# A two-block model on one core: the weight units moved to other byte phases, the memory's additions and transposes placed further apart

## The reference

```python
def hybrid_layer(x, mem_n, ...):            # twice
    h = layer_norm(ALPHA * x + 0.5 * swiglu(x, ffn1_w_gu, ffn1_w_down), ln_g[0], ln_b[0])
    (dn_q, dn_k, dn_v, dn_b, dn_a, dn_z, sw_q, sw_k, sw_v, xa_q, gates) = split(h @ w_in)
    o_dn = deltanet_branch(...)             # chunked gated delta rule, 4 heads of 128
    o_sw = sliding_window_attention(sw_q, sw_k, sw_v, swa_sinks)
    o_xa = memory_cross_attention(xa_q, mem_n, w_mem_kv)
    merged = sum(sigmoid(gates) * (branches @ w_branch))
    h = layer_norm(ALPHA * h + merged @ w_out, ln_g[1], ln_b[1])
    return layer_norm(ALPHA * h + 0.5 * swiglu(h, ffn2_w_gu, ffn2_w_down), ln_g[2], ln_b[2])

def first_block(x, mem, ...):
    mem_n = layer_norm(mem, mem_ln_g, mem_ln_b)          # 256 x 1024
    for l in range(2): x = hybrid_layer(x, mem_n, ...)

def second_block(x, ...):                   # once
    x = x + token_mixer(rmsnorm(x, g), ...) # four attention variants, gates, w_out
    x = x + conv_ffn(rmsnorm(x, g), ...)    # 1024 -> 5632 -> 1024
    return rmsnorm(x, norm_final_g)
```

## Time and profile before

| | |
|---|---|
| time, median of 3 runs | 3506.49 us (3505.77 to 3510.85) |
| the profiled execution's own time | 3508.38 us, granted clock 0.997 |
| its span | 3506.6 us |
| PE busy | 3446.7 us (98%), 19244 matmuls |
| DVE, ACT busy | 2226.2 us (63%), 1676.8 us (48%) |
| DMA | 358.88 MB, mean 102 GB/s |

### The profile page before, as it was taken

The page is one execution under the profiler, slowest core; times in us unless marked ns, Lnnn a source line. Parts: engine busy times, 40 slices in busy tenths (PEclk is TensorE's granted clock), DMA queues, the critical chain, the costliest instruction groups (busy, mean ns, idle before and its releaser), DMA issues.

```text
span 3506.6 us, 49704 instructions
## 1 busy us (share of the span) xinstructions
PE 3446.7 (98%) x19244; PEld 2934.4 (84%) x19244; DVE 2226.2 (63%) x4226; ACT 1676.8 (48%) x3230; POOL 111.5 (3%) x132
## 2 busy tenths in 40 slices
PE   9999999999999999999999999999999999999999
PEld 7998888877889998999888877888987777788887
DVE  5566565556685667566755566774766777666653
ACT  5355454554354445444555544453545444444432
POOL 0010000000000100010000000000100000000000
PEclk9999999999999999999999999999999999999999
DMA  5464321112334643464221112254632222233332
GB/s 154 134 172 148 121 88 52 45 52 64 97 99 135 172 130 104 131 168 136 91 72 46 46 58 84 94 136 137 168 118 76 67 70 82 73 96 96 97 99 88
DMA packets 197140, 358.88 MB, mean 102 GB/s; under 512 B 21982, under 2 KB 25215, under 8 KB 196904
## 3 DMA queue, kind: packets, MB, share of 16 engines
q1 hardware_dynamic: 177704, 321.34, 29.1%
q0 software_dynamic: 18432, 33.56, 5.7%
q10 hardware_dynamic: 768, 0.79, 0.1%
HBM read 353.23 MB, written 4.74 MB: 102 GB/s over the span
## 4 chain that ended last, share of the span: by engine, by line
PE 90%; DVE 6%; ACT 3%; issue 1%; DMA 0%; DVEq 0%; SPq 0%; ACTq 0%
PE bank L2491 20%; PE bank L2500 20%; PE bank L2492 20%; PE bank L2526 6%; PE bank L2529 6%; PE bank L2528 6%; PE bank L2479 2%; PE bank L2474 1%; PE bank L2569 1%; PE bank L2662 1%; DVE w_lo L3235 1%; PE bank L2672 1%; DVE page_r L3277 1%; PE bank L2537 1%; PE bank L2589 1%
## 5 line engine op out<-in xcount | busy, mean ns | idle before, releaser
L2491 PE MATMUL bank<-page_r,w_hi 128*128 128x512 f32 (+1 forms) x3446 | 1368.2, 397 | 27.7 <-DVE w_lo L3235 21.9
L2500 PE MATMUL bank<-page_r,w_lo 128*128 128x512 f32 (+1 forms) x3446 | 1343.8, 390 | 0.0
L2492 PE MATMUL bank<-page_r,w_hi 128*128 128x512 f32 (+1 forms) x3446 | 1332.4, 387 | 0.0
L2491 PEld LDWEIGHTS bank<-page_r,w_hi 128*128 128x128 f32 x3446 | 650.0, 189 | 174.5 <-DVE w_lo L3235 23.1
L2815 ACT ACTIVATE w_hi<-raw 128x512 fp32r<-128x512 f32 x864 | 532.4, 626 | 515.0 <-PE bank L2500 506.7
L2500 PEld LDWEIGHTS bank<-page_r,w_lo 128*128 128x128 f32 x3446 | 649.4, 188 | 129.0
L2492 PEld LDWEIGHTS bank<-page_r,w_hi 128*128 128x128 f32 x3446 | 650.2, 189 | 125.6 <-issue 3.8
L3235 DVE TENSOR_TENSOR w_lo<-raw,w_hi 128x512 fp32r<-128x512 f32 x864 | 574.6, 686 | 141.1 <-ACT w_hi L2815 139.1
L2526 PE MATMUL bank<-page_r,w_hi 128*128 128x256 f32 x1792 | 507.3, 283 | 2.4 <-DVE w_lo L3253 2.4
L2528 PE MATMUL bank<-page_r,w_hi 128*128 128x256 f32 x1792 | 507.1, 283 | 0.0
L2529 PE MATMUL bank<-page_r,w_lo 128*128 128x256 f32 x1792 | 507.1, 283 | 0.0
(11 more groups left out here) (321 smaller groups left out, 3437.4 us busy)
## 6 DMA issues: line engine op xcount, KB each, us to landing
raw<-weights SPq DMA_DIRECT2D x864, 256.0 KB, 2.6
raw<-pairs SPq DMA_DIRECT2D x320, 256.0 KB, 3.1
raw<-pairs POOLq DMA_DIRECT2D x128, 256.0 KB, 5.8
bias_rows<-bias_row SPq DMA_DIRECT2D x8, 320.0 KB, 4.4
page_f<-x_t SPq DMA_DIRECT2D x8, 256.0 KB, 5.5
page_f<-bias_rows SPq DMA_DIRECT2D x8, 256.0 KB, 4.6
out_t<-page_f SPq DMA_DIRECT2D x12, 128.0 KB, 1.8
cst<-consts SPq DMA_DIRECT2D x4, 272.0 KB, 3.6
```

The source lines that it names most:

```text
L2491: self.e.matmul(o, hi, X.hi[kt], start=first, stop=False)
L2492: self.e.matmul(o, hi, X.lo[kt], start=False, stop=False)
L2500: last = self.e.matmul(o, lo, X.hi[kt], start=False, stop=final)
```

## The change

Three things. First, units get 32 floats between them (`PITCH`), `small` shrinks to make room, and each unit is placed when it is taken: a slab's unit at the start of its pitch plus 28 floats, plus 32 more where its number is odd; a unit of a Strassen pair at plus 20 floats; a unit lent as a page at plus 0. The room shifts the pages too: they now start at phase 0. All slab units start at phase 240 (16 bytes short of a page's phase), pair units at phase 64 or 192. The wide instructions on two units now have two runs of 512 with a gap. Second, the layer norm of the memory yields twice after each of its seven additions, and each value projection waits six steps instead of one between its copy and its transposes. Third, the bias row is written from two pages by two DMAs.

```diff
+SMALL = 1184
+UNIT_START = 28
+SLAB_PHASE = (0, 32)
+PAIR_PHASE = 20
 CONST_PARTS = 4
 NGAIN = 48
 UNIT = SLAB * P
+PITCH = UNIT + 32
...
-        super().__init__(region[:, at * UNIT:(at + 1) * UNIT], rounded[:, at * UNIT:(at + 1) * UNIT])
+        super().__init__(None)
         self.at, self.region, self.rounded, self.landed, self.loads = at, region, rounded, landed, 0
         self.added, self.adds = added, 0
+        self.place(0)
+
+    def place(self, phase):
+
+        self.phase, a = phase, UNIT_START + self.at * PITCH + phase
+        self.f, self.r = self.region[:, a:a + UNIT], self.rounded[:, a:a + UNIT]
+        return self
+
+    def for_slab(self):
+
+        return self.place(SLAB_PHASE[self.at % 2])
+
+    def for_pair(self):
+
+        return self.place(PAIR_PHASE)
+
+    def two(self, region):
+        a = UNIT_START + self.at * PITCH
+        both = region[:, a:a + 2 * PITCH].rearrange("p (u c) -> p u c", u=2)
+        return both[:, :, self.phase:self.phase + UNIT]
 
     def wide(self):
-        return self.region[:, self.at * UNIT:(self.at + 2) * UNIT]
+        return self.two(self.region)
 
     def wide_rounded(self):
-        return self.rounded[:, self.at * UNIT:(self.at + 2) * UNIT]
+        return self.two(self.rounded)
...
-            slot = lender.take()
+            slot = lender.take().place(0)
...
-        with nc.sbuf_tensor("w_lo", [P, NRAW * UNIT], F32R) as lo:
+        with nc.sbuf_tensor("w_lo", [P, NRAW * PITCH + 64], F32R) as lo:
             self.w_lo = lo
-        self.raw = sb("raw", [P, NRAW * UNIT])
-        with nc.sbuf_tensor("w_lent", [P, NHI * UNIT], F32) as lent:
+        self.raw = sb("raw", [P, NRAW * PITCH + 64])
+        with nc.sbuf_tensor("w_lent", [P, NHI * PITCH + 32], F32) as lent:
             self.w_lent = lent
-        self.w_hi = sb("w_hi", [P, NHI * UNIT], F32R)
+        self.w_hi = sb("w_hi", [P, NHI * PITCH + 32], F32R)
...
-        self.small = sb("small", [P, 2048])
+        self.small = sb("small", [P, SMALL])
...
-            unit = self.raws.take()
+            unit = self.raws.take().for_slab()
...
-            raw, hi = self.slab[self.next_round] = [self.slab[self.next_round][0], self.his.take()]
+            raw, hi = self.slab[self.next_round] = [self.slab[self.next_round][0], self.his.take().for_slab()]
...
-        k.will(vector="s1 s2 s3 s4 s5 s6 s7")
-        self.tiles_sum(k, s, tiles, landed, n)
+        for m in range(1, 8):
+            k.will(vector=f"s{m}")
+            self.tiles_sum(k, s, tiles, landed, n, m)
+            yield
+            yield
         for _ in range(6):
...
-        out = s1, s3 = self.raws.take_pair()
+        out = s1, s3 = [x.for_pair() for x in self.raws.take_pair()]
...
                         self.memory_out(k, b, q, 0)
                         self.banks.give(b, k["out"])
-                        yield
+                        for _ in range(6):
+                            yield
...
-        self.bias_store(k, row)
+        self.bias_store(k, p, p2)
+        self.pages.give(p, (self.m.s_row, 32))
+        self.pages.give(p2, (self.m.s_row, 32))
...
-    def tiles_sum(self, k, s, tiles, landed, n):
-        self.clear(s)
-        self.wait_ge(*landed[0])
-        self.wait_ge(*landed[1])
-        self.e.tensor_tensor(s.cols(n), tiles[0].cols(n), tiles[1].cols(n), ALU.add).then_inc(k.lane.vector, 1)
-        for m in range(2, 8):
-            self.wait_ge(*landed[m])
+    def tiles_sum(self, k, s, tiles, landed, n, m):
+        self.wait_ge(*landed[m])
+        if m == 1:
+            self.clear(s)
+            self.wait_ge(*landed[0])
+            self.e.tensor_tensor(s.cols(n), tiles[0].cols(n), tiles[1].cols(n), ALU.add).then_inc(k.lane.vector, 1)
+        else:
             self.wait_ge(*k[f"s{m - 1}"])
             self.e.tensor_tensor(s.cols(n), s.cols(n), tiles[m].cols(n), ALU.add).then_inc(k.lane.vector, 1)
...
+        self.wait_ge(*k["wide"])
+        self.e.dma_start(self.m.row[:, 0:SEQ], p.f[0:8, :]).then_inc(self.m.s_row, 16)
         self.wait_ge(*k["narrow"])
-        self.e.dma_start(self.m.row, row[0:8, :]).then_inc(self.m.s_row, 16)
+        self.e.dma_start(self.m.row[:, SEQ:640], p2.f[0:8, 0:P]).then_inc(self.m.s_row, 16)
```

More of the change, by code:

```diff
@@ L538, in small @@
         self.small_at += n
-        assert a + n <= 2048
+        assert a + n <= SMALL
         return self.m.small[:, a:a + n]
@@ L916, in prepare @@
         add("a11", s3)
-        a11 = self.raws.take()
+        a11 = self.raws.take().for_pair()
         load("a11", a11)
         yield
-        a12, a22 = self.raws.take_pair()
+        a12, a22 = [x.for_pair() for x in self.raws.take_pair()]
         load("a12", a12)
@@ L923, in prepare @@
         yield
-        s2, s4 = self.raws.take_pair()
+        s2, s4 = [x.for_pair() for x in self.raws.take_pair()]
         k.will(vector="second")
         self.sum_second(p, s1, a11, s2)
-        h11 = self.his.take()
+        h11 = self.his.take().for_pair()
         k.will(scalar="h11")
@@ L932, in prepare @@
         yield
-        h13 = self.his.take_pair()
+        h13 = [x.for_pair() for x in self.his.take_pair()]
         k.will(scalar="h13")
@@ L940, in prepare @@
         self.rest_units(p, out, h13, k["h13"])
-        h24 = self.his.take_pair()
+        h24 = [x.for_pair() for x in self.his.take_pair()]
         k.will(scalar="h24")
@@ L946, in prepare @@
         yield
-        h12, h22 = self.his.take_pair()
+        h12, h22 = [x.for_pair() for x in self.his.take_pair()]
         k.will(scalar="h12")
@@ L1592, in bias_rows @@
         k = self.marks("rows")
-        o0, o1, row = self.pages.take(), self.pages.take(), self.small(640)
+        o0, o1, p, p2 = (self.pages.take() for _ in range(4))
         self.bias_start(o0, o1)
@@ L1598, in bias_rows @@
         k.will(tensor="rows", scalar="wide narrow")
-        self.bias_matmul(k, o0, o1, b, b2, row)
+        self.bias_matmul(k, o0, o1, b, b2, p, p2)
         self.banks.give(b, k["wide"])
@@ L2719, in finish_sum, with bias_matmul @@
         self.e.matmul(b.cols(SEQ), self.const("ones"), q.cols(SEQ), start=True, stop=True).then_inc(k.lane.tensor, 1)
-    def bias_matmul(self, k, o0, o1, b, b2, row):
+    def bias_matmul(self, k, o0, o1, b, b2, p, p2):
         self.clear(b)
@@ L3149, in output_gate, with bias_matmul @@
         self.e.activation(z.f[:, :], b.f[:, :], ACT.Tanh, scale=0.5).then_inc(k.lane.scalar, 1)
-    def bias_matmul(self, k, o0, o1, b, b2, row):
+    def bias_matmul(self, k, o0, o1, b, b2, p, p2):
+        self.clear(p)
         self.wait_ge(*k["rows"])
-        self.e.activation(row[0:8, 0:SEQ], b.f[0:8, :], ACT.Copy).then_inc(k.lane.scalar, 1)
-        self.e.activation(row[0:8, SEQ:640], b2.f[0:8, 0:P], ACT.Copy).then_inc(k.lane.scalar, 1)
+        self.e.activation(p.f[0:8, :], b.f[0:8, :], ACT.Copy).then_inc(k.lane.scalar, 1)
+        self.clear(p2)
+        self.e.activation(p2.f[0:8, 0:P], b2.f[0:8, 0:P], ACT.Copy).then_inc(k.lane.scalar, 1)
     def stick_scores(self, k, i, rows, b, z, s, q, keys):
@@ L3825, in bias_start, with bias_store @@
         self.e.dma_start(o1.f[0:33, 0:128], self.m.buckets[:, 512:640]).then_inc(self.m.s_onehot, 16)
-    def bias_store(self, k, row):
+    def bias_store(self, k, p, p2):
+        self.wait_ge(*k["wide"])
+        self.e.dma_start(self.m.row[:, 0:SEQ], p.f[0:8, :]).then_inc(self.m.s_row, 16)
         self.wait_ge(*k["narrow"])
-        self.e.dma_start(self.m.row, row[0:8, :]).then_inc(self.m.s_row, 16)
+        self.e.dma_start(self.m.row[:, SEQ:640], p2.f[0:8, 0:P]).then_inc(self.m.s_row, 16)
     def bias_spread(self, h):
-        self.wait_ge(self.m.s_row, 16)
+        self.wait_ge(self.m.s_row, 32)
         self.e.dma_start(self.m.scratch[h], self.m.row[h:h + 1, :].broadcast_to([P, 640])).then_inc(self.m.s_rows[h], 16)
```

## The result

The changed kernel takes 3471.09 us (median of 4, 3469.10 to 3474.11) against 3508.26 us for the kernel before on the same chip: ratio 0.9898, 95% interval 0.9884 to 0.9913, so 37 us or 1.0% faster. The forecast was 3436 us, 2.0% faster. The sign was right, and the time lies in the range; the size was half. The profiled execution took 3474.11 us, 34.3 us less than that of before.

The account below looks back on a forecast made before the run. PE was taken as the bound, through matmul count times distance between starts. Gains of 27 (slabs), 36 (pairs), 3.4 and 3.6 us (memory) sum to 70 off 3508.4, forecast 3436 us after adjusting to the median; range 3350 to 3515.

Parts of the forecast that it names:

- Pairs: 256-column matmuls on Strassen pairs, units moved to phase 64 or 192: 6.7 ns less each, 36 us gained.
- the surplus: Distance between matmul starts beyond the stream's own time at 2.4 GHz: 13.3 ns with 512 columns and with 256.
- rival A: The forecast itself: new phases ease a conflict between weight load and streaming read; 3395 to 3485 us, chance 0.45.
- Slabs: 512-column slab matmuls, weights moved to phase 240 with pages at 0: 2.7 ns less each, 27 us gained.
- (c): Around the load of mean_rounded, 32 bytes out of phase, three distances average 233 ns against 226.7: not a fixed cost.
- rival D: New phases meet worse: slab matmuls at 233 ns, costing 63 us, 3562 us in all; chance 0.17.
- Rival C: The phases do nothing; only the memory's 7 us remain, 3499.5 us; chance 0.22.
- B: Conflict between load and stream gone in slabs and pairs: 3320 us at the least, about 3380 with two thirds; chance 0.12.
- E: DMA landings or wide instructions so late that PE waits in Strassen stages: 19 us and more, 3518 and above; chance 0.04.
- Memory: Waits at the memory's layer norm additions and ahead of its transposes shrink: 3.4 and 3.6 us gained.
- the squares: In the memory's layer norm, six of eight matmuls on squares come three blocks after the mean, possibly late: 1 us charged.
- Costs at nothing: Wide remainders' split pattern, DMAs to 16-byte addresses and the bias row's second DMA: 0; wide remainders uncovered at most 19 us.

Follow-up runs that it names:

- the map: Separate kernel without the model: stretches of 48 matmuls, weights at 16 phases against the page; 226.67 to 234.25 ns with 512 columns, 113.33 to 120.04 with 256.

## Where the prediction failed, and where it held

**Pairs: right in size, with luck in it.** -36 us forecast, -34.6 measured, and undoing it alone gives 26 us of time back. The distance came to 113.6 ns, the 113.3 that half the surplus would make. That the phase matters, as rival A had it, is shown; that the load and the stream meet better, its reason, is not. The size rested on the 0.11 of the earlier trace rows, which is 114 ns to the nanosecond, and "half the surplus" was a choice: phase 64 can also settle at 117.8, and all other phases on the map lie between 116.7 and 120. At 117.8 the pairs would have given 12 us.

**Slabs: the step that failed.** "I take -2.7 ns, a fifth of the surplus, because it is inside the reading nearest to a better case, the 0.22 of the earlier trace rows". The measured value was +0.7 ns, and 27 us of gain became 6.6 of loss; the 34 us between them are nearly the whole miss. That 0.22 is the difference of two times rounded to 10 ns: the trace has 228 ns there, more than the steady 226.7. A 224 does stand nearby once, between a 236 and a 231, but no placing holds it: over 256 the least steady distance is 226.6. The prediction itself said that no row showed a 512-column stream that did better, and that (c) was the only sight of another phase. (c) pointed the right way: `mean_rounded` lies at relative phase 224, for which the map has 233.33. The 233 read off is rounding too, though: to the nanosecond the three distances are 227, 235 and 232, 231 on average, and the next is 226 again. Taken as the only data for slabs, it puts their term at 0 or above. At 0 the sum is -43 us, 3463, close to what the kernel takes with slabs left in phase (3463.95), though the memory gave 3.5 us more than its terms and the pairs 1.4 less. By the prediction's own sign ("wrong in the main if the slab distance is still 226.7 ns") it failed in the first stretch shown, and in the second, at 9.59 us, by that of rival D.

**Rival D** (a worse phase) had the slabs' direction right and the size wrong here: its 6.3 ns are about what most phases do, 64 among them, and 240 happens to be one of the few that cost at most 1.7. Had the slabs gone to 64 and 192 it would have been 37 us of time, nearly all of the gain. **Rival C** is refuted, **B** too: nothing comes near 213.3 ns. **E** did not occur: landings grew by 0.1 and 0.4 us, and DVE waited 23 us more for them, but PE only 0.5 more for DVE. The addresses are not what made them longer, for the kernel with the memory alone, whose units lie as before, has 2.7 and 3.5 us as well.

**Memory: mechanism right, too small.** -3.4 and -3.6 forecast, -10.5 measured. The transposes gave 4.0. The additions gave 3.1 + 1.4 + 2.0: the 0.6 that I kept for waiting was 0.2, the 1.7 for half clock was 0.3 too much, the 1 us charged for the squares did not come, and the remainder that was late 18 us further on stood in the earlier trace rows as an idle time of 2.0 that the sum left out.

**Costs at nothing: right**, by the wide remainder at 1218 ns and PE's waits at the pair products, 2.9 us against 2.4. The 0.05 us an instruction that bounds the cost stands in no row; it measured -0.001.

The account: pairs -34.6, memory -10.5, slabs +6.6 make -38.5; the medians differ by 37.2 and the profiled executions by 34.3. Most of the rest is in stretches at half clock that come and go. The changed kernel's profile has two of 3.4 us that the profile before has not, up to 1.7 us lost in each:

```profile
804.60:808.00 3.40, 3.40 (x10) 2.62 (x9) 3.08 (x16) 0.00 (x0) 0.00 (x0) 0.50 0.00 0
2057.20:2060.60 3.40, 3.40 (x8) 2.75 (x9) 3.12 (x14) 0.00 (x0) 0.00 (x0) 0.51 0.00 0
```

Another instance, engines' busy time and the clock (the third figure from the end), in the kernel before and in the one with the memory alone at the same work:

```profile
2690.00:2700.00 10.00, 10.00 (x45) 7.53 (x44) 5.67 (x14) 4.71 (x12) 0.00 (x0) 0.80 0.08 29
```

```profile
2679.60:2689.60 10.00, 10.00 (x52) 7.83 (x51) 6.31 (x15) 4.72 (x12) 0.00 (x0) 1.00 0.14 34
```

The instructions are the same; the kernel before has 45 matmuls in 10 us and the other 52. Such stretches moved the difference of these two traces by 1.6 or 3.2 us at a time, in either direction; a median evens them out better than a single profile.

## What to carry to other kernels

Where float32r matmuls follow each other with their own weight loads, the phase of the stationary tile against the moving one, modulo 256 bytes, is worth 3% of the distance with 512 columns and 6% with 256, and the best phase differs by shape: here 0 for 512 columns and 64 for 256. Don't infer it from a rounded distance in an unsettled row: a kernel of some sixty stretches measures the map in one run, and the map then predicted two edits of a 3.5 ms kernel to within 8 us. Measure a phase more than once, since it can settle at more than one distance. And where an engine's burst makes PE wait once, look for a second wait behind it.

## What the runs showed that I had not expected

- The same instructions at the same addresses have more than one steady distance: 226.67 or 228.33 ns at phase 240, 113.33 or 117.78 ns for 256 columns at 64. With nothing between the stretches, what ran before decided it.
- Shifts of 4, 8 and 12 bytes cost about as much as larger ones (512 columns: 232.3, 230.7, 230.0 ns against 226.67 at 0 and at 16), so floats off by one are not harmless. Shifts of 256 and 320 bytes behave as 0 and 64.
- A four times narrower weight tile does not shorten the distance of 512 columns: 230 to 232 ns, more than the full tile's 226.67 at phase 0.
